# Attention scores two heads ahead of the turned probabilities, rows turned three heads ahead, same buffers

## The reference, cut to what matters

```
def causal_block_attention(q_nope, q_rope, k_nope, k_rope, v):
    ...
        s = einsum(q_nope, k_nope) + einsum(q_rope, k_rope)     # 64 + 32 columns of a head
        s = s * scale
        p = softmax(where(mask, s, -inf))                       # over the keys, causal
        outs.append(einsum(p, v))
    ...
q = (rms_norm(cq, g_q) @ w_uq)            # 16 heads x 96; its last 32 columns are rotated
o = o * silu(gate);  return o @ w_out     # gate: 1024 columns of h @ w_in
```

## Time and profile before

| | |
|---|---|
| median of three runs | 942.67 us (942.47 to 942.71) |
| the profiled execution | 942.05 us, of which its span 940.3 us |
| TensorE busy | 914.9 us, 97% of the span |
| VectorE, ScalarE, GpSimd busy | 596.6 us (63%), 474.5 us (50%), 124.5 us (13%) |
| the loop over the 16 heads | about 259 to 326 us |

### The profile page before, as it was taken

How to read it: one execution, slowest core, us unless ns; L and a number is a source line. 1 busy time by engine, 2 the same in 40 slices (tenths; PEclk the granted TensorE clock), 3 DMA queues, 4 the chain that set the end, 5 groups by cost and what they waited for, 6 DMA issues and landing times.

```text
span 940.3 us, 13508 instructions
## 1 busy us (share of the span) xinstructions
PE 914.9 (97%) x4998; PEld 770.6 (82%) x4998; DVE 596.6 (63%) x1057; ACT 474.5 (50%) x764; POOL 124.5 (13%) x100
## 2 busy tenths in 40 slices
PE   9999999999999999999999999999999999999996
PEld 6999878889888868888788888877978788888885
DVE  3798465776767687677765554567486865545455
ACT  5755756556676444772453433425574354334430
POOL 5553773101000010001100000000001100000001
PEclk9999999999999999999999999999999999999998
DMA  8754232473525118233465455443432265454511
GB/s 315 263 181 157 90 135 90 145 258 137 215 99 180 45 57 343 71 124 119 161 230 216 180 179 189 173 174 141 173 135 90 90 226 217 173 190 179 195 73 46
DMA packets 22237, 151.74 MB, mean 161 GB/s; under 512 B 2593, under 2 KB 2977, under 8 KB 4257
## 3 DMA queue, kind: packets, MB, share of 16 engines
q1 hardware_dynamic: 20160, 142.62, 42.0%
q10 hardware_dynamic: 2016, 8.29, 2.4%
HBM read 149.85 MB, written 1.05 MB: 160 GB/s over the span
## 4 chain that ended last, share of the span: by engine, by line
PE 82%; DVE 8%; ACT 3%; issue 3%; POOL 2%; DMA 1%; POOLq 0%; DVEq 0%; ACTq 0%; SPq 0%
PE ps L510 15%; PE ps L512 15%; PE ps L516 15%; PE ps L1113 5%; PE ps L541 3%; PE ps L545 3%; PE ps L543 3%; PE ps L789 2%; PE ps L791 2%; PE ps L790 2%; PE ps L561 2%; PE ps L1131 2%; PE ps L680 2%; PE ps L683 1%; PE ps L682 1%
## 5 line engine op out<-in xcount | busy, mean ns | idle before, releaser
L1294 ACT CAST whi<-raw 128x2048 fp32r<-128x2048 f32 x127 | 242.0, 1913 | 146.0 <-PE ps L516 112.3
L1759 DVE TENSOR_TENSOR wlo<-raw,whi 128x1024 fp32r<-128x1024 f32 x127 | 166.0, 1307 | 142.7 <-ACT whi L1294 142.4
L510 PE MATMUL ps<-whi,ahi 128*128 128x512 f32 (+2 forms) x448 | 173.6, 387 | 0.8 <-issue 0.7
L512 PE MATMUL ps<-wlo,ahi 128*128 128x512 f32 (+2 forms) x448 | 171.7, 383 | 0.0
L516 PE MATMUL ps<-whi,alo 128*128 128x512 f32 (+2 forms) x448 | 170.7, 384 | 0.0
L1765 DVE TENSOR_TENSOR wlo<-raw,whi 128x1024 fp32r<-128x1024 f32 x106 | 129.1, 1218 | 0.0
L510 PEld LDWEIGHTS ps<-whi,ahi 128*128 128x128 f32 x448 | 84.2, 188 | 18.5 <-issue 2.5
L516 PEld LDWEIGHTS ps<-whi,alo 128*128 128x128 f32 x448 | 84.2, 188 | 16.4
L512 PEld LDWEIGHTS ps<-wlo,ahi 128*128 128x128 f32 x448 | 84.2, 188 | 16.3 <-issue 0.5
L541 PE MATMUL ps<-ahi,whi 128*128 128x256 f32 x256 | 73.4, 287 | 0.6 <-POOL wlo L2443 0.6
L543 PE MATMUL ps<-alo,whi 128*128 128x256 f32 x256 | 72.4, 283 | 0.0
(11 more groups left out here) (284 smaller groups left out, 1710.5 us busy)
## 6 DMA issues: line engine op xcount, KB each, us to landing
raw<-in_wstream SPq DMA_DIRECT2D x134, 1024.0 KB, 4.8
par<-in_params ACTq DMA_DIRECT2D x5, 1024.0 KB, 4.7
tab<-in_tables ACTq DMA_DIRECT2D x1, 1370.0 KB, 8.3
res<-in_x SPq DMA_DIRECT2D x2, 512.0 KB, 4.4
out<-res SPq DMA_DIRECT2D x4, 256.0 KB, 2.1
par<-in_params ACTq DMA_DIRECT2D x1, 512.0 KB, 3.3
arena<-in_wf ACTq DMA_DIRECT2D x2, 256.0 KB, 5.1
arena<-in_wsmall ACTq DMA_DIRECT2D x1, 256.0 KB, 8.4
```

Of the source, the lines that this page charges most:

```text
L510: pe.matmul(banks[b][:, 0:cw], h_, wh[:, i, c], start=st, stop=False, skip_group_check=True)
L512: pe.matmul(banks[b][:, 0:cw], h_, wl[:, i, c], start=False, stop=False, skip_group_check=True)
L1294: act.copy(whi[:, u % SPL, :], raw[:, u % RAW, :]).then_inc(w_hi, 1)
L1759: dve.tensor_tensor(wlo[:, u % SPL, c], raw[:, u % RAW, c], whi[:, u % SPL, c].bitcast(F32), ALU.subtract).then_inc(w_lo_v, 1)
```

## The change

`mla_turn` goes three heads ahead of `mla_pt` instead of two, and `mla_scores` two instead of one, on TensorE, in ScalarE's copies and in the plan of fills. `mla_exp(1)` goes ahead of ScalarE's loop, and in the loop `mla_exp(h + 2)` stands behind the parts' copies and ahead of the weight split. On VectorE `mla_max(1)` goes ahead of the loop, and `mla_max(h + 2)` stands behind `mla_pt_out(h)`, where `mla_max(h + 1)` stood ahead of it. `A_PIECES`, `A_SPLITS`, `Q_ROTATED_AT` and the slots of all buffers stay as they are.

```diff
@@ fill_plan
-    plan += [(("qk", 0), "a"), (("qk", 1), "a")]
+    plan += [(("qk", 0), "a"), (("qk", 1), "a"), (("qk", 2), "a")]
     for h in range(MH):
-        if h + 2 < MH:
-            plan += [(("qk", h + 2), "a")]
+        if h + 3 < MH:
+            plan += [(("qk", h + 3), "a")]
@@ TensorE
             mla_scores(0)
+            mla_turn(2)
+            mla_scores(1)
             for h in range(MH):
-                if h + 2 < MH:
-                    mla_turn(h + 2)
+                if h + 3 < MH:
+                    mla_turn(h + 3)
                 if h in O_TURNED_AT:
                     o_turn(O_TURNED_AT[h])
-                if h + 1 < MH:
-                    mla_scores(h + 1)
+                if h + 2 < MH:
+                    mla_scores(h + 2)
@@ ScalarE
             mla_exp(0)
+            mla_qk(2)
+            mla_exp(1)
             for h in range(MH):
-                if h + 2 < MH:
-                    mla_qk(h + 2)
+                if h + 3 < MH:
+                    mla_qk(h + 3)
                 if h in O_TURNED_AT:
                     halves_hi(("o", O_TURNED_AT[h]), ahi, 2 * O_TURNED_AT[h])
-                if h + 1 < MH:
-                    mla_exp(h + 1)
...
+                if h + 2 < MH:
+                    mla_exp(h + 2)
                 if h in A_SPLITS:
                     split.until(A_SPLITS[h], 0)
@@ VectorE
             mla_max(0)
+            mla_max(1)
             for h in range(MH):
-                if h + 1 < MH:
-                    mla_max(h + 1)
                 if h in O_TURNED_AT:
                     halves_lo(("o", O_TURNED_AT[h]), ahi, alo, 2 * O_TURNED_AT[h])
                 mla_pt_out(h)
+                if h + 2 < MH:
+                    mla_max(h + 2)
```

## The result

The changed kernel took 946.1 us, the median of six executions (945.72 to 947.32), against 942.69 us before (942.32 to 942.99, six as well). The ratio is 1.0039, with a 95% interval of 1.0027 to 1.0051: slower by 3.4 us, where 4.4 had been forecast. TensorE's busy time is 1.4 us of 915 longer.

What follows compares the result with a forecast made beforehand. TensorE, busy 97% of the span, was taken as the bound, so only its stops count. Terms of 1.9 + 1.9 - 0.15 + 0.55 + 0.2 gave 4.4 us slower, 947.0 us from 942.67, range 944.8 to 949.2.

Steps and rivals of the forecast that it cites:

- The walk through the queues: Head loop: following TensorE, ScalarE and VectorE in the new order gives old time less six stops plus the new ones.
- Step A: Loop start: `mla_scores(2)` waits for ScalarE's copy `mla_qk(2)` behind `mla_exp(0)` and its table load; loss 1.9 us.
- Step B: Fifth head: `mla_turn(5)`, now opening iteration 2, waits for VectorE's `q_rotate(1, 1)`; loss 1.9 us.
- Step C: Split of gate 3 on ScalarE, now behind `mla_exp(4)`: stop 0.6 us before `mla_turn(7)`, a gain of 0.15.
- Step D: Heads 7 to 9: `mla_pv(8)` waits for `gate_second` behind one more max, 6.2 us after `mla_pt(7)`; net loss 0.55.
- Step E: Heads 9 to 12: `mla_pt(11)` waits for `mla_qk(14)`, loss 1.2 us, plus 0.2 and 0.3 later; net loss 0.2.
- The sum: Whole run: 1.9 + 1.9 - 0.15 + 0.55 + 0.2 = 4.4 us slower, from 942.67 to 947.0.
- No slack takes the delay up: Behind the loop: everything hangs on `mla_pv(15)` and TensorE is full, so the loop's delay stays in the total.
- The first two: Rivals: early losses small and late stops gone, 940.5, 4%; or early losses as forecast and late stops gone, 943.6, 9%.
- The second's sum: Rival with early losses as forecast and late stops gone: 4.4 - 0.75 - 2.75 = 0.9, giving 943.6; 9%.
- The third, the clock: Rival: TensorE's clock falls to 1.2 GHz after an early stop, 3 to 6 us of matmuls doubled, 950 to 953; 4%.

## Why the prediction was right

- **The walk through the queues** held. TensorE's work is unchanged, and the loop grew by 4.52 us, against 4.4.
- **Step A**: printed 1.77 us, with the 0.16 that a stop costs beyond it 1.93, against 1.9. The table load took 1.28 us again and the exponentials began 0.01 us behind it (261.66 and 262.95), so no drain was added. Undoing the step gave 2.07 back.
- **Step B**: 1.75 and 0.16, against 1.9. Its end was the rotation, as said; but I had not looked for what was second in that wait, and undoing it gave 1.37, as had been worked out before that run.
- **Step C**: 0.42 and 0.16, against 0.6, and released by ScalarE's copy.
- **Step D**: `mla_pv(8)` started 6.27 us after `mla_pt(7)` (302.16), against 6.2. The reason given for the net loss, the one max put ahead of the gate, is not a cause whose removal helps: the swap back made the loop 0.5 longer.
- **Step E**: `mla_pt(11)` started 5.34 us after `mla_pv(8)`, 4.2 of them work: 1.1 lost, against 1.2; 0.2 and 0.3 more behind it, as said.
- **The sum was 1.0 us too high in the total**, because the end of the program was taken as it was. "No slack takes the delay up" is right for TensorE; 1.11 us came from the place where the last instructions are fetched, of which the profile of before had only the packet behind the output's. The 0.42 us behind the loop, which the sum had at nothing, went the other way and stays unexplained.
- **The rivals.** The first two are out: both early stops and the late ones are there. (The second's sum takes the late stops off twice: with A and B at 3.8 and all others gone, 3.5, it is 0.3 and not 0.9, so 943.0; nothing hangs on it.) The third, the clock, had 4% and happened in 6 of 11 executions of the changed kernel. Its mechanism was right and both numbers were wrong: the chance too small, and the price, behind which no row stood, too large (1.5 us for a fall, not 3 to 6). The argument against it, "no more than 2 us, and matmuls before and behind", did not hold. That the time stayed in the range in spite of it is luck: a fall costs little, and the slower executions took 947.1 to 948.1.

## What to carry to other kernels

When a step is moved ahead in a queue that is full, write down for each instruction that moves what releases it and what covered that wait before; a prologue and the first iterations pay for a longer lead, because there the producers have no lead of their own. A longer lead through the same number of slots gained nothing here: the max could not start before its slot was free, and the loop was 1.1 us slower even with the early stops mended, while moving weight splits out of the stretch in which VectorE is full won 1.8 us. Where two kernels differ by a few tenths of a per cent, split the run into stretches of the bottleneck engine before believing a total: here an end 1.1 us shorter hid a quarter of the loop's loss.

## What the runs showed of the hardware

- Stops of TensorE of 1.8 us, with matmuls before and behind, were followed in a part of the executions by a fall of its clock to 1.2 GHz. In the two profiles that show it, the fall came about 1 us after the first stop had ended, eight matmuls of 128x512 were 0.43 us apart instead of 0.23, and 1.54 us were lost. With the stops removed there was no slower execution in 11, and with matmuls that nothing reads placed in them none in 5, at no cost. Whether a given execution falls was not settled; it varied from 2 of 6 to 4 of 5 for one kernel.
- One VectorE instruction more, in a wait, made the program 1.1 us shorter behind the last matmul (7.85 against 8.96 us) and 1.3 us in the median, with a fetch of instructions ahead of the output's transfer and not behind it. Which engine's code that packet holds the traces don't say.
